# The eight experts of a routed layer: the next expert's tokens gathered one expert ahead, and its first product drawn before the last transposes

## The chip, the cores and the metric

The kernel runs on 1 core of one Trainium2 chip. The metric is device time in microseconds (us). The kernel before takes 2135.12 us, the median of 3 runs (2126.69 to 2139.0).

## The reference

The program is a trunk of two layers on 256 tokens of width 1024, batch 1, in float32. Each layer has a token-mixing half (not touched here) and a channel-mixing half. In layer 0 the latter is a dense SwiGLU; in layer 1 it is routed, and this is where the change lies:

```python
def swiglu(h, w1, w3, w2):
    return (jax.nn.silu(h @ w1) * (h @ w3)) @ w2

def moe_ffn(h, w_router, w1, w3, w2):
    logits = (h @ w_router).astype(jnp.float32)
    top_v, top_i = lax.top_k(logits, TOP_K)          # 2 of 8
    top_w = jax.nn.softmax(top_v, axis=-1)
    gate = jnp.sum(one_hot(top_i, N_EXPERTS) * top_w[..., None], axis=-2)
    y = jnp.zeros_like(h)
    for e in range(N_EXPERTS):
        y = y + gate[..., e:e + 1] * swiglu(h, w1[e], w3[e], w2[e])
    return y
```

Each expert has w1 and w3 of 1024 x 3584 and w2 of 3584 x 1024, in float32: 42 chunks of 1 MiB.

## The kernel before

Each expert works on at most 128 tokens, gathered by a product with a one-hot matrix `sel` (tokens x slots). If an expert is chosen by more than 128 tokens, a second round over all experts follows; in this run there is none, so the expert loop runs 8 times.

**Precision.** Every float32 product is made of three fp32r products: operands are split into a high part (rounded copy, ScalarE, line 1234) and a low part (the difference, VectorE). `mm3` (lines 677 to 679) issues xl·wh, xh·wl, xh·wh. So every weight passes over ScalarE and VectorE once.

**Weights.** SyncE loads chunks of 1 MiB into the ring `raw` of 6 (line 539), each as soon as the chunk six earlier is split. A chunk has two halves of 128x1024. ScalarE copies a half to `w_hi`, VectorE then writes `w_lo` (line 1568); both are rings of 4 halves, so half h can be split only when TensorE has used half h-4 (`half_used`). The splits are written into each engine's instruction order by `use(n)`: it splits up to 3 halves (`AHEAD`) beyond the chunks it takes, then the engine goes on with its other work. ScalarE and VectorE run in their own written order, and whatever stands in it between two splits delays the later one.

**An expert.** Its width 3584 is walked in 7 blocks of 512. The gate product G of a block takes 4 chunk halves (24 matmuls of 128x512) into bank `pA[0]`, the up product U as many into `pA[2]`, the down product 4 halves into the two banks `pO`, in which all 7 blocks accumulate. `silu` (ScalarE, line 1520) reads `pA[0]` into `a_sb`, `hidden` (VectorE, line 2081) multiplies `pA[2]` in, `turn_a` transposes `a_sb` with 4 small matmuls (line 725) into the two banks `pT`, and these are split to `aT_hi`, `aT_lo` (line 2089). Banks `pA[1]` and `pA[3]` are idle in the expert loop.

TensorE's order in one expert is: transpose `sel` to `selT`; open the output banks with a product of zeros; G(0), U(0); then six times G(f), turn_a(f-1), U(f), down(f-1); then `gather` for the next expert (32 matmuls of 128 columns into both `pT`, line 682); turn_a(6); down(6); and the scatter, `selT` times the output `oe` (4 products of 128x512 into `pT`, line 682, each shown as two records).

VectorE's part of it: `one_hot` (line 2051) makes `sel` of the next expert after its first `hidden`; `gathered` (line 2060) scales the gathered tokens out of the banks into `x_f` in 8 instructions, followed by a drain (line 2063); ScalarE and VectorE split `x_f` into `x_hi` and `x_lo` (line 2068); `oe` is copied out half by ScalarE and half by VectorE (line 2109); and four instructions add the scattered rows to `yacc` (line 2114).

Of the kernel before, what the change touches and what calls it, by code (L numbers as in the profile page):

```python
# [31 lines left out]
P = 128  # L32
D = 1024
# [288 lines left out]
def build(nc, a, table, out):  # L322
    ctx = ExitStack()
    with ctx:
# [97 lines left out]
        sel = sb("sel", [P, TT, P], at=work + 20480)  # L422
        selT = sb("selT", [P, TT * P], at=work + 21504)
# [90 lines left out]
        x_ready = sem("x_ready")  # L514
        fin_ready = sem("fin_ready")
# [11 lines left out]
        def _(sp):  # L527
# [56 lines left out]
            for l in range(DEPTH):  # L584
# [37 lines left out]
                else:  # L622
                    def experts():
                        with rounds(sp, 0, NE, {b.raw: EFB * 6}) as e:
                            w1, w3, w2 = (a[n][l // 2].rearrange("e k n -> (e k) n") for n in ("moe_w1", "moe_w3", "moe_w2"))

                            def up(f0):
                                for w in (w1, w3):
                                    for k in range(2):
                                        load(chunk_rows(w, e * D + k * CK * P, f0))  # L630

                            def down(f0):
                                for half in range(2):
                                    load(chunk_rows(w2, e * FFE + f0, half * W))
# [9 lines left out]
                    items = sp.value_load(flag[0:1, 0:1], min_val=NE, max_val=2 * NE)  # L644
                    with sp.If(items > NE):
                        experts()
# [9 lines left out]
        def _(pe):  # L656
# [333 lines left out]
            for l in range(DEPTH):  # L990
# [109 lines left out]
                else:  # L1100
# [16 lines left out]
                    items = pe.value_load(flag[0:1, 0:1], min_val=NE, max_val=2 * NE)  # L1117
                    evacuated(b.A, A_free, 4)
                    G, U, av, xv = Turn(start=FFB + 1), Turn(start=FFB + 1), Turn(start=FFB + 1), Turn()
# [10 lines left out]
                    pe.wait_ge(sel_ready, 2)  # L1130
                    gather()
                    with rounds(pe, 0, items, {b.raw: 42, b.hl: 84, b.T: 22, b.O: 2, G: EFB, U: EFB, av: EFB, xv: 1}):
                        v = xv.take()
                        for t in range(TT):
                            turned([sel[:, t, :]], P)
                        outs = [take_O(), take_O()]
                        for o in outs:
                            mm(o[:, :].rearrange("p (k n) -> p k n", k=CK), zeros[:, :],
                               zeros[:, :].unsqueeze(1).broadcast_to([P, CK, P]), True, False)
                        pe.wait_ge(x_ready, xv.done(v, 2))  # L1140

                        def gate_up(dst, turn, free):
                            v = turn.take()
                            pe.wait_ge(free, turn.done(v - 1))
                            product([dst], lambda j, t: (x_hi[:, j, :], x_lo[:, j, :]), 2)

                        def turn_a():
                            v = av.take()
                            pe.wait_ge(a_ready, av.done(v))
                            for q in range(2):  # L1150
                                turned([a_sb[:, 0, (2 * q + j) * P:(2 * q + j + 1) * P] for j in range(2)], P)

                        def down(last=False):
                            evacuated(b.T, T_free, 2)
                            for half in range(2):
                                for i in range(2):
                                    wh, wl = half_in(i)
                                    for j in range(CK // 2):
                                        k = i * (CK // 2) + j
                                        ins = mm3(outs[half][:, :], aT_hi[:, k, 0:P], aT_lo[:, k, 0:P],  # L1160
                                                  wh[:, j * W:(j + 1) * W], wl[:, j * W:(j + 1) * W], False, last and k == CK - 1)
                                    ins.then_inc(half_used, 1)
                        gate_up(pA[0], G, g_free)
                        gate_up(pA[2], U, u_free)
                        with rounds(pe, 1, EFB, {b.raw: 6, b.hl: 12, b.T: 2, G: 1, U: 1, av: 1}):
                            gate_up(pA[0], G, g_free)
                            turn_a()
                            gate_up(pA[2], U, u_free)
                            down()
                        pe.wait_ge(sel_ready, xv.done(v) + 2)  # L1170
                        gather()
                        turn_a()
                        down(True)
                        evacuated(b.O, O_free, 2)
                        for t in range(TT):
                            for half in range(2):
                                dst = take_T()
                                mm(dst[:, :], selT[:, t * P:(t + 1) * P], oe[:, half * W:(half + 1) * W]).then_inc(T_full, 1)

# [43 lines left out]
        def _(act):  # L1223
# [27 lines left out]
            def start_splits():  # L1251

                b.end = 2 * (DEPTH * MIX_CHUNKS + DENSE_CHUNKS + 6 * EFB)
# [146 lines left out]
            for l in range(DEPTH):  # L1400
# [97 lines left out]
                else:  # L1498
# [4 lines left out]
                    items = act.value_load(flag[0:1, 0:1], min_val=NE, max_val=2 * NE)  # L1503
                    G, xv = Turn(start=FFB + 1), Turn()

                    def hi_x(at):
                        for q in range(2):
                            act.wait_ge(xf_ready, at + q + 1)
                            copy(x_hi[:, 4 * q:4 * q + 4, :], x_f[:, 4 * q:4 * q + 4, :]).then_inc(x_hi_ready, 1)
                    skip(b.T, 2)  # L1510
                    hi_x(0)
                    with rounds(act, 0, items, {b.raw: 42, b.hl: 84, b.hl_in: 84, b.T: 22, b.O: 2, G: EFB, xv: 1}) as e:
                        v = xv.take()
# [3 lines left out]
                        def silu():  # L1517
                            G.take()
                            act.wait_ge(half_used, b.hl.done(b.hl.n - 1))
                            nc.scalar.activation(a_sb[:, 0, :], pA[0][:, :], ACT.Silu).then_inc(g_free, 1)  # L1520

                        def hi_a():
                            for q in range(2):
                                pt, free = T_in()
                                copy(aT_hi[:, 2 * q:2 * q + 2, 0:P], pt[:, 0:SEQ].rearrange("p (k n) -> p k n", k=2)).then_inc(aT_hi_ready, 1)
# [3 lines left out]
                        with rounds(act, 1, EFB, {b.raw: 6, b.hl: 12, b.hl_in: 12, b.T: 2, G: 1}):  # L1529
                            use(2)  # L1530
                            hi_a()
                            silu()
                            use(4)
                        skip(b.T, 2)
                        hi_a()
                        hi_x(xv.done(v, 2))
                        u = use(2)
                        with act.If(e < items - 1):
                            ahead()
                        act.wait_ge(half_used, b.hl.done(u))  # L1540
                        copy(oe[:, 0:W], pO[b.O.slot(b.O.take())][:, :]).then_inc(O_free[0], 1)
                        skip(b.O, 1)
                        skip(b.T, 4)
# [4 lines left out]
        def _(dve):  # L1548
# [42 lines left out]
            def start_splits():  # L1591

                b.end = 2 * (DEPTH * MIX_CHUNKS + DENSE_CHUNKS + 6 * EFB)
# [286 lines left out]
            for l in range(DEPTH):  # L1880
# [127 lines left out]
                else:  # L2008
# [32 lines left out]
                    link(V.tensor_scalar(r(9)[:, 1:2], r(9)[:, 0:1], float(P), float(NE), ALU.is_gt, ALU.mult))  # L2041
                    link(V.tensor_scalar(flag[:, 0:1], r(9)[:, 1:2], float(NE), None, ALU.add))
                    link(V.memset(slot16[:, :, 2 * NE:], -1.0))
                    dve.drain().then_inc(slots_ready, 1)
                    items = dve.value_load(flag[0:1, 0:1], min_val=NE, max_val=2 * NE)
                    av, aq, xv = Turn(start=FFB + 1), Turn(start=2 * FFB + 1), Turn()

                    def one_hot(e):

                        for t in range(TT):  # L2050
                            ins = V.tensor_scalar(sel[:, t, :], iota, slot16[:, t, bass.ds(e, 1)], None, ALU.is_equal)
                        ins.then_inc(sel_ready, 1)

                    def gathered():

                        for q in range(2):
                            pt, free = T_in()
                            for j in range(4):
# [85 lines left out]
```

## Time and profile before

| | |
|---|---|
| profiled execution | 2136.17 us, its span 2134.4 us |
| busy share of the span | PE 93%, PEld 74%, VectorE (DVE) 72%, ScalarE (ACT) 58%, GpSimd (POOL) 4% |
| mean granted TensorE clock | 0.962 of full speed |
| read from HBM | 530.83 MB, 249 GB/s over the span |
| expert phase | from 1024.1 us (first `sel`) to about 2120 us |

PE is TensorE's matmuls, PEld its weight loads. Busy shares are over the whole span. A matmul's record is longer than the distance to the next one, since matmuls overlap in the pipeline, so distances between starts tell the pace. In the timeline, one row can stand for several instructions of a kind (x4), and its duration is from the first start to the last end. What stands in square brackets is idle time of the engine ahead of the row and the engine and line that ended it; DVEq is VectorE's sequencer (here the drain), "issue" means that the profile shows nothing that was waited for.

### The profile page before, as it was taken

The page shows a single profiled execution, that of the slowest core. Times are in us where ns is not written, and L with a number is a line of the kernel's source. Part 1 is how long each engine was busy: PE and PEld are TensorE (multiplying, and loading weights), DVE is VectorE, ACT ScalarE, POOL GpSimd, SP SyncE. Part 2 cuts the span into 40 slices and gives each one's busy share as a digit, 9 for nine tenths or more (in the row PEclk, how much of TensorE's full clock was granted, in tenths as well). Part 3 has the DMA queues.
Part 4 walks back from the last instruction along what each step waited for, and adds up shares of the span by engine and source line. Part 5 has one row for each costly group of instructions (what it writes and reads, how often), then busy time and mean ns, then how long its engine had stood idle before and what let it go on. Part 6 is the DMA issues. An engine that isn't in the chain of part 4 may idle for free.

```text
span 2134.4 us, 28418 instructions
## 1 busy us (share of the span) xinstructions
PE 1991.8 (93%) x9524; PEld 1576.0 (74%) x9524; DVE 1526.7 (72%) x1827; ACT 1237.3 (58%) x1590; POOL 90.3 (4%) x133
## 2 busy tenths in 40 slices
PE   5999999899979999997899999999999999999996
PEld 2777887777767777886686886877868778687785
DVE  2654565654556644656787897988979888798887
ACT  2544454344324544542576876767767677677773
POOL 0510100000003300000000000000000000000000
PEclk7999999899988999998899999999999999999998
DMA  9656545355734655353597997989979989799892
GB/s 324 218 199 216 179 136 160 115 201 186 257 110 157 234 184 216 119 177 99 189 364 275 352 367 260 363 307 316 365 256 365 328 298 366 258 365 345 289 366 101
DMA packets 275180, 532.74 MB, mean 250 GB/s; under 512 B 10720, under 2 KB 23216, under 8 KB 274992
## 3 DMA queue, kind: packets, MB, share of 16 engines
q1 hardware_dynamic: 275120, 531.91, 71.1%
q8 instruction: 41, 0.67, 0.1%
q14 instruction: 19, 0.16, 0.0%
HBM read 530.83 MB, written 1.05 MB: 249 GB/s over the span
## 4 chain that ended last, share of the span: by engine, by line
PE 84%; DVE 8%; ACT 3%; issue 2%; DVEq 2%; SPq 1%; DMA 0%; ACTq 0%
PE pA L677 17%; PE pA L679 17%; PE pA L678 17%; PE pO L682 6%; PE pO L677 6%; PE pO L679 6%; PE pO L678 6%; PE pT L725 4%; PE pT L682 4%; DVE w_lo L1568 2%; ACT w_hi L1234 1%; PE pA L682 1%; SPq L539 1%; DVE yacc L2114 1%; DVEq L2082 1%
## 5 line engine op out<-in xcount | busy, mean ns | idle before, releaser
L1568 DVE TENSOR_TENSOR w_lo<-raw,w_hi 128x1024 fp32r<-128x1024 f32 x914 | 1093.7, 1225 | 311.5 <-ACT w_hi L1234 290.6
L1234 ACT ACTIVATE w_hi<-raw 128x1024 fp32r<-128x1024 f32 x914 | 957.1, 1058 | 566.8 <-PE pA L679 425.0
L677 PE MATMUL pA<-w_hi,x_lo 128*128 128x512 f32 x896 | 360.3, 402 | 1.7 <-DVE x_lo L2068 0.8
L679 PE MATMUL pA<-w_hi,x_hi 128*128 128x512 f32 x896 | 354.3, 395 | 0.0
L678 PE MATMUL pA<-w_lo,x_hi 128*128 128x512 f32 x896 | 354.0, 395 | 0.0
L677 PE MATMUL pA<-w_hi,h_lo 128*128 128x512 f32 (+2 forms) x736 | 300.2, 408 | 8.3 <-DVE w_lo L1568 8.3
L678 PE MATMUL pA<-w_lo,h_hi 128*128 128x512 f32 (+2 forms) x736 | 290.3, 394 | 0.0
L679 PE MATMUL pA<-w_hi,h_hi 128*128 128x512 f32 (+2 forms) x736 | 289.9, 394 | 0.0
L677 PE MATMUL pO<-w_hi,aT_lo 128*128 128x512 f32 x536 | 218.5, 408 | 19.3 <-DVE yacc L1976 8.8
L678 PE MATMUL pO<-w_lo,aT_hi 128*128 128x512 f32 x536 | 216.4, 404 | 0.0
L679 PE MATMUL pO<-w_hi,aT_hi 128*128 128x512 f32 x536 | 216.3, 404 | 0.0
L677 PEld LDWEIGHTS pA<-w_hi,x_lo 128*128 128x128 f32 x896 | 168.4, 188 | 45.3 <-DVE w_lo L1568 4.4
L679 PEld LDWEIGHTS pA<-w_hi,x_hi 128*128 128x128 f32 x896 | 168.5, 188 | 40.8
L678 PEld LDWEIGHTS pA<-w_lo,x_hi 128*128 128x128 f32 x896 | 168.6, 188 | 37.3
L677 PEld LDWEIGHTS pA<-w_hi,h_lo 128*128 128x128 f32 x736 | 142.6, 194 | 52.9 <-issue 18.8
L679 PEld LDWEIGHTS pA<-w_hi,h_hi 128*128 128x128 f32 x736 | 142.3, 193 | 31.8
L678 PEld LDWEIGHTS pA<-w_lo,h_hi 128*128 128x128 f32 x736 | 142.8, 194 | 27.9
L677 PEld LDWEIGHTS pO<-w_hi,aT_lo 128*128 128x128 f32 x536 | 103.8, 194 | 48.0 <-DVE w_lo L1568 10.8
L679 PEld LDWEIGHTS pO<-w_hi,aT_hi 128*128 128x128 f32 x536 | 103.6, 193 | 25.4
L678 PEld LDWEIGHTS pO<-w_lo,aT_hi 128*128 128x128 f32 x536 | 103.9, 194 | 24.5
L1234 ACT ACTIVATE aT_hi<-pT 128x256 fp32r<-128x256 f32 (+1 forms) x123 | 43.8, 401 | 77.3 <-PE pT L725 77.3
L682 PE MATMUL pO<-raw,csilu 128*32 128x512 f32 x384 | 52.9, 665 | 7.4 <-DMA raw<-in_ada_w 7.4
(228 smaller groups left out, 1713.7 us busy)
## 6 DMA issues: line engine op xcount, KB each, us to landing
raw<-in_moe_w SPq DMA_DIRECT2D x336, 1024.0 KB, 6.8
raw<-in_w_in SPq DMA_DIRECT2D x56, 1024.0 KB, 5.9
raw<-in_ada_w SPq DMA_DIRECT2D x48, 1024.0 KB, 9.3
raw<-in_ffn_w SPq DMA_DIRECT2D x33, 1024.0 KB, 6.2
raw<-in_w_out SPq DMA_DIRECT2D x8, 1024.0 KB, 5.1
raw<-in_cmp_k_w SPq DMA_DIRECT2D x4, 1024.0 KB, 5.3
raw<-in_cmp_v_w SPq DMA_DIRECT2D x4, 1024.0 KB, 10.3
raw<-in_w_read_nsa SPq DMA_DIRECT2D x4, 1024.0 KB, 8.4
```

The lines of the kernel that those rows point to most:

```text
L539: sp.dma_start(slot[:, 0:kb * src.shape[2]].rearrange("p (k n) -> p k n", k=kb), src).then_inc(landed[b.raw.slot(g)], 16)
L677: nc.tensor.matmul(dst, xl, wh, start=first, stop=False, skip_group_check=True)
L678: nc.tensor.matmul(dst, xh, wl, start=False, stop=False, skip_group_check=True)
L679: return nc.tensor.matmul(dst, xh, wh, start=False, stop=last, skip_group_check=True)
L682: return nc.tensor.matmul(dst, lhsT, rhs, start=first, stop=last, skip_group_check=True)
L725: ins = nc.tensor.transpose(pt[0:m, i * width:i * width + n], src, ident[0:n, 0:n])
L1234: return nc.scalar.activation(dst, src, ACT.Copy)
L1568: V.tensor_tensor(w_lo[m][:, 0:n], raw[s][:, i * n:(i + 1) * n], w_hi[m][:, 0:n].bitcast(F32), ALU.subtract).then_inc(raw_done, 1)
L2082: dve.drain().then_inc(u_free, 1)
L2114: V.scalar_tensor_tensor(dst, pt[:, :], gate16[:, t, bass.ds(e, 1)], dst, ALU.mult, ALU.add).then_inc(free, 1)
```

## The change

1. TensorE's order. `gather` writes `pA[1]` and `pA[3]` with semaphores of its own, is done one expert further ahead, and stands behind the last down product and ahead of the scatter. The next expert's G(0) stands ahead of turn_a(6), its U(0) behind it: the end of an expert has the same order as any other block. Transposing `sel` and opening the output banks come behind the scatter.
2. `sel` is needed while `gather` is an expert ahead, so there is a second one-hot matrix `sel_s` for the scatter, made by two more VectorE instructions per expert.
3. The splits of the next expert's tokens (`hi_x`, `lo_x`) come behind the U product of block 6, ahead of the splits of the chunks that follow.
4. SyncE loads the next expert's first four chunks ahead of the last two of the present one.
5. The loops: one over passes (one or two), in it one over 7 experts, and the last expert by itself. The branch with which ScalarE and VectorE ended each expert is left only behind the last. In every expert the last of the six blocks stands outside the inner loop.

```diff
@@ SyncE
-                            up(0)
-                            with rounds(sp, 1, EFB, {b.raw: 6}) as f:
-                                up(f * W)
-                                down(f * W - W)
-                            down((EFB - 1) * W)
+                        up(0, 0)
+                        with rounds(sp, 0, NE - 1, {b.raw: EFB * 6}) as e:
+                            blocks(e)
+                            up(e + 1, 0)
+                            down(e, (EFB - 1) * W)
+                        blocks(NE - 1)
+                        down(NE - 1, (EFB - 1) * W)
...
@@ TensorE
                     def gather():
+                        v = gv.take()
+                        pe.wait_ge(sel_ready, gv.done(v) + 1)
+                        pe.wait_ge(gather_free, gv.done(v - 1))
                         for q in range(2):
-                            pt = take_T()
...
-                                    ins = mm(pt[:, j * P:(j + 1) * P], y[:, t, k * P:(k + 1) * P], sel[:, t, :], t == 0, t == 1)
-                            ins.then_inc(T_full, 1)
+                                    ins = mm(pA[1 + 2 * q][:, j * P:(j + 1) * P], y[:, t, k * P:(k + 1) * P], sel[:, t, :], t == 0, t == 1)
+                            ins.then_inc(gather_full, 1)
...
+                        gather()
+                        first_block()
+                        gate_up(pA[2], U, u_free)
+                        gather()
+                        turn_sel()
+                        with rounds(pe, 0, NE - 1, {...}):
+                            blocks()
+                            first_block()
+                            turn_a()
+                            gate_up(pA[2], U, u_free)
+                            down(True)
+                            gather()
+                            scatter()
+                            turn_sel()
+                        blocks()
+                        turn_a()
+                        down(True)
+                        scatter()
...
@@ ScalarE
+                    def hi_x():
+                        v = gv.take()
+                        act.wait_ge(half_used, b.hl.done(b.hl.n - 1))
+                        for q in range(2):
+                            act.wait_ge(xf_ready, gv.done(v, 2) - 1 + q)
+                            copy(x_hi[:, 4 * q:4 * q + 4, :], x_f[:, 4 * q:4 * q + 4, :]).then_inc(x_hi_ready, 1)
...
+                    def block():
+                        use(2)
+                        hi_a()
+                        silu()
+                        use(2)
+
+                    def blocks(more):
+                        with rounds(act, 1, EFB - 1, {...}):
+                            block()
+                            use(2)
+                        block()
+                        if more:
+                            hi_x()
+                        use(2)
...
+                        hi_x()
+                        use(2)
+                        silu()
+                        use(2)
+                        keep_sel()
+                        with rounds(act, 0, NE - 1, {...}):
+                            blocks(True)
+                            block()
+                            use(2)
+                            outs()
+                            keep_sel()
+                        blocks(False)
+                        hi_a()
+                        use(2)
...
@@ VectorE
+                    def blocks(more):
+                        with rounds(dve, 1, EFB - 1, {...}):
+                            block()
+                            use(2)
+                        block()
+                        if more:
+                            lo_x()
+                        return use(2)
...
+                        one_hot(sel, p * NE, sel_ready)
+                        one_hot(sel_s, p * NE, sel_s_ready)
+                        gathered()
+                        one_hot(sel, p * NE + 1, sel_ready)
+                        lo_x()
+                        use(2)
+                        use(2)
+                        hidden()
+                        gathered()
...
+                        with rounds(dve, 0, NE - 1, {...}) as e:
+                            at = p * NE + e
+                            one_hot(sel, at + 2, sel_ready)
+                            dve.wait_ge(T_full, b.T.done(b.T.n - 1))
+                            one_hot(sel_s, at + 1, sel_s_ready)
+                            blocks(True)
+                            block()
+                            outs(use(2))
+                            gathered()
+                            scattered(at)
+                            skip(b.T, 2)
+                        blocks(False)
+                        lo_a()
+                        v = use(2)
...
+                        outs(v)
+                        scattered(p * NE + NE - 1)
```

`block`, `outs` and `scattered` hold the same instructions as before: `block` is the splits, `lo_a` or `hi_a`, and `hidden` or `silu`; `outs` the copy into `oe`; `scattered` the four additions.

## Rows read from the trace of the kernel before

**Rows 1.** What TensorE waited for, 1120 to 2134 us: total us, times, longest.

```profile
PE pT L725 <- DVEq L2063: 10.3, 8, 1.3
```

**Rows 2.** Timeline of TensorE, end of one expert, and next expert's gather: start, duration.

```profile
1284.70 3.73 PE L682 MATMUL pT<-sel,y 128*128 128x128 f32 x32
...
1291.39 0.79 PE L677 MATMUL pO<-w_hi,aT_lo 128*128 128x512 f32 x1 [1.01 <-DVE aT_lo L2089]
...
1294.89 0.39 PE L679 MATMUL pO<-w_hi,aT_hi 128*128 128x512 f32 x1
...
1298.39 0.40 PE L679 MATMUL pO<-w_hi,aT_hi 128*128 128x512 f32 x1
1300.44 4.02 PE L682 MATMUL pT<-oe,selT 128*128 128x512 f32 x8 [1.66 <-issue]
...
1305.87 0.50 PE L677 MATMUL pA<-w_hi,x_lo 128*128 128x512 f32 x1
...
1420.98 3.73 PE L682 MATMUL pT<-sel,y 128*128 128x128 f32 x32
```

**Rows 3.** Timeline of TensorE inside an expert, around the first transposes.

```profile
1184.85 0.40 PE L679 MATMUL pA<-w_hi,x_hi 128*128 128x512 f32 x1
1185.36 0.50 PE L677 MATMUL pA<-w_hi,x_lo 128*128 128x512 f32 x1
...
1186.87 0.60 PE L725 MATMUL pT<-tab,a_sb 128*128 128x128 f32 x4
...
1187.54 0.39 PE L678 MATMUL pA<-w_lo,x_hi 128*128 128x512 f32 x1
```

**Rows 4.** Timeline of all engines, 1148 to 1170 us, the expert before that.

```profile
1148.65 3.73 PE L682 MATMUL pT<-sel,y 128*128 128x128 f32 x32
1150.64 1.37 DVE L2060 TENSOR_SCALAR x_f<-pT,mod 128x128 f32<-128x128 f32 x4 [0.87 <-PE pT L682]
...
1152.43 1.36 DVE L2060 TENSOR_SCALAR x_f<-pT,mod 128x128 f32<-128x128 f32 x4 [0.42 <-PE pT L682]
...
1163.40 0.68 DVE L2109 COPY oe<-pO 128x512 f32<-128x512 f32 x1
...
1166.23 0.30 PEld L682 LDWEIGHTS pT<-oe,selT 128*128 128x128 f32 x2 [0.93 <-DVE yacc L2114]
...
1167.52 1.49 DVE L2114 SCALAR_TENSOR_TENSOR yacc<-pT,gate,yacc 128x512 f32<-128x512 f32 x2 [0.59 <-PE pT L682]
...
1169.57 0.51 PE L677 MATMUL pA<-w_hi,x_lo 128*128 128x512 f32 x1
```

**Rows 5.** Timelines of ScalarE and VectorE in a block in mid-expert.

```profile
1257.26 3.06 ACT L1234 ACTIVATE w_hi<-raw 128x1024 fp32r<-128x1024 f32 x3
...
1262.06 1.06 ACT L1234 ACTIVATE w_hi<-raw 128x1024 fp32r<-128x1024 f32 x1 [0.34 <-PE pA L679]
...
1262.91 0.68 DVE L2081 TENSOR_TENSOR a_sb<-a_sb,pA 128x512 f32<-128x512 f32 x1
1263.86 4.72 DVE L1568 TENSOR_TENSOR w_lo<-raw,w_hi 128x1024 fp32r<-128x1024 f32 x4 [0.26 <-issue]
```

**Rows 6.** Timeline ahead of the first expert's first product: tokens' low part.

```profile
1031.98 1.29 DVE L2068 TENSOR_TENSOR x_lo<-x_f,x_hi 128x512 fp32r<-128x512 f32 x2
```

**Rows 7.** Windows: length, busy us by engine, PEclk, DMA share, GB/s.

```profile
1152.20:1155.30 3.10, 0.85 (x6) 0.37 (x4) 2.21 (x6) 1.31 (x4) 0.00 (x0) 0.93 0.58 218
1155.30:1158.00 2.70, 2.66 (x6) 2.16 (x7) 2.52 (x3) 1.43 (x2) 0.00 (x0) 0.50 0.01 4
...
1162.40:1169.60 7.20, 4.92 (x14) 1.79 (x13) 4.67 (x6) 2.33 (x4) 0.00 (x0) 1.00 0.50 155
...
1180.00:1276.00 96.00, 95.89 (x424) 77.23 (x423) 86.98 (x88) 75.85 (x85) 0.00 (x0) 1.00 1.02 363
```

**Rows 8.** ScalarE's line 1520 from 1010 us on: duration min/median/max, first and last start.

```profile
L1520 ACT ACTIVATE a_sb<-pA x56: 597/606/609, 1040.4 to 2090.1; 128x512 f32<-128x512 f32 x56
L1520 ACT ACT_TABLE_LOAD  x8: 1283/1283/1283, 1039.1 to 1991.2; - x8
```

More of the change, by code:

```diff
@@ new lines, in gather, with turn_sel, gate_up @@
+                            ins.then_inc(gather_full, 1)
+                    def turn_sel():
+                        pe.wait_ge(sel_s_ready, sv.done(sv.take()))
+                        for t in range(TT):
+                            turned([sel_s[:, t, :]], P)
+                    def gate_up(dst, turn, free):
+                        v = turn.take()
+                        pe.wait_ge(free, turn.done(v - 1))
+                        product([dst], lambda j, t: (x_hi[:, j, :], x_lo[:, j, :]), 2)
@@ new lines, in first_block, with turn_a, down @@
+                    def first_block():
+                        pe.wait_ge(x_ready, xv.done(xv.take(), 2))
+                        gate_up(pA[0], G, g_free)
+                    def turn_a():
+                        v = av.take()
+                        pe.wait_ge(a_ready, av.done(v))
+                        for q in range(2):
+                            turned([a_sb[:, 0, (2 * q + j) * P:(2 * q + j + 1) * P] for j in range(2)], P)
+                    def down(last=False):
+                        evacuated(b.T, T_free, 2)
+                        for half in range(2):
+                            for i in range(2):
+                                wh, wl = half_in(i)
+                                for j in range(CK // 2):
+                                    k = i * (CK // 2) + j
+                                    ins = mm3(outs[half][:, :], aT_hi[:, k, 0:P], aT_lo[:, k, 0:P],
+                                              wh[:, j * W:(j + 1) * W], wl[:, j * W:(j + 1) * W], False, last and k == CK - 1)
+                                ins.then_inc(half_used, 1)
@@ L1138, in _, with open_outs @@
+                    def open_outs():
+                        for _ in range(2):
+                            o = take_O()
                             mm(o[:, :].rearrange("p (k n) -> p k n", k=CK), zeros[:, :],
                                zeros[:, :].unsqueeze(1).broadcast_to([P, CK, P]), True, False)
[L1140 to L1162, printed above, removed]
+                    def block():
@@ L1172, in _, with blocks, scatter @@
-                        turn_a()
-                        down(True)
+                        down()
+                    def blocks():
+                        open_outs()
+                        with rounds(pe, 1, EFB - 1, {b.raw: 6, b.hl: 12, b.T: 2, G: 1, U: 1, av: 1}):
+                            block()
+                        block()
+                    def scatter():
                         evacuated(b.O, O_free, 2)
@@ L1514, in _, with silu @@
                         for t in range(TT):
                             T_copy(lambda pt: (selT[:, t * P:(t + 1) * P], pt[:, 0:P]))
[L1517 to L1525, printed above, removed]
+                    def silu():
+                        G.take()
+                        act.wait_ge(half_used, b.hl.done(b.hl.n - 1))
+                        nc.scalar.activation(a_sb[:, 0, :], pA[0][:, :], ACT.Silu).then_inc(g_free, 1)
@@ new lines, in gathered, with lo_x, hidden @@
+                        dve.drain().then_inc(gather_free, 1)
+                    def lo_x():
+                        v = xv.take()
+                        for q in range(2):
+                            dve.wait_ge(x_hi_ready, xv.done(v, 2) - 1 + q)
+                            V.tensor_tensor(x_lo[:, 4 * q:4 * q + 4, :], x_f[:, 4 * q:4 * q + 4, :],
+                                            x_hi[:, 4 * q:4 * q + 4, :].bitcast(F32), ALU.subtract).then_inc(x_ready, 1)
+                    def hidden():
+                        v = av.take()
+                        dve.wait_ge(g_free, av.done(v))
+                        dve.wait_ge(half_used, b.hl.done(b.hl.n - 1))
+                        V.tensor_tensor(a_sb[:, 0, :], a_sb[:, 0, :], pA[2][:, :], ALU.mult).then_inc(a_ready, 1)
+                        dve.drain().then_inc(u_free, 1)
@@ L2094, in _ @@
[L2094 to L2095 removed]
+                    def blocks(more):
+                        with rounds(dve, 1, EFB - 1, {b.raw: 6, b.hl: 12, b.hl_in: 12, b.T: 2, av: 1, aq: 2}):
+                            block()
                             use(2)
[L2097 to L2100 removed]
@@ L2101, in _, with outs @@
-                        gathered()
-                        lo_a()
-                        lo_x(xv.done(xe, 2))
-                        v = use(2)
-                        with dve.If(e < items - 1):
-                            ahead()
+                        block()
+                        if more:
+                            lo_x()
+                        return use(2)
+                    def outs(v):
                         b.O.take()
```

173 lines of the change are left out of this document (79 added, 94 removed).

## The prediction

> **What bounds the kernel now.** I read the page first, then the waits of TensorE, then the timelines around one expert's end, then windows. In the expert phase TensorE is the bound: in 96 us inside an expert it is busy 95.89 us at full clock, with VectorE at 91% of that window, ScalarE at 79%, and DMA moving 363 GB/s at a busy share of 1.02 [rows 7]. The reader should see two things there: only what lies on TensorE's line at an expert's end can be won, and the three others have little room for what the change pushes beside the products. In mid-stream the pace is one 128x512 matmul each 0.2333 us (15 steps from 1294.89 to 1298.39) [rows 2]; I use this pace, not the 0.40 us of a record, because records overlap.
>
> From one gather to the next an expert takes 1420.98 - 1284.70 = 136.28 us [rows 2]. It splits up as:
> - products: 84 halves x 6 matmuls x 0.2333 = 117.6 us;
> - six turn_a inside blocks: from 1186.87 to 1187.54 less one step, 0.44 each [rows 3], 2.6 us;
> - **gap A**, gather and turn_a(6), 1291.39 - 1284.70 = 6.7 us [rows 2]. One wait in it is on VectorE's drain behind `gathered`, since gather and turn_a share both `pT`; 8 of these are 10.3 us [rows 1];
> - **clock**: in 1152.2 to 1155.3, within such a gap, TensorE is busy 0.85 of 3.1 us, and the 2.7 us behind it are granted 0.50, the 1.2 GHz level [rows 7]. The first 8 steps of down(6) take 3.50 us in place of 1.87 [rows 2]: 1.6 us;
> - **gap B**, scatter, turned `sel`, opened banks: from 1298.62 to 1305.87, 7.25 us [rows 2]. No fall of the clock follows it although TensorE is busy for only 4.92 of 7.2 us (granted 1.00) [rows 7];
> - a stall at the first U, 1185.36 against 1185.08 due, 0.3 us [rows 3], and 0.1 for the first step after a pause.
>
> The sum is 136.3, so nothing large is missing.
>
> **Gap A goes.** G(0) of the next expert stands ahead of turn_a(6) and U(0) behind it, as in every block, so turn_a(6) should cost the 0.44 us of the others, its copies hidden by the 5.6 us of U(0). Its products are only moved.
>
> **Gap B grows by the gather.** I count from the end of down(6). TensorE gathers until 3.6 (3.73 less the overlap into the next start [rows 2]). VectorE, beside it: splits behind, then the `oe` copy from 1.05 to 1.75 (1163.40, gap B of that expert having begun 7.25 ahead of 1169.57 [rows 4]). `gathered` starts 2.0 after the gather (1150.64 against 1148.65) and runs 1.37, its second half starts at 3.8 (1152.43) and ends at 5.15 [rows 4]; some 0.3 for the drain, by the 0.26 behind `hidden` [rows 5]: 5.45. Only now can VectorE add the scattered rows, because they are queued behind `gathered`. TensorE has put two scatter products into the two `pT` by then; the third needs the first bank. Addition one ends at 6.2 and the third product starts (as 1166.23 in the old order). The third addition starts 1.3 after that (1167.52) and the last ends at 9.05, and the next product starts 0.56 later, as 1169.57 does behind 1167.52 + 1.49 [rows 4]. So the new gap is 9.6 us. Lower bound 9.0: gather 3.6 and the old 1305.87 - 1300.44 = 5.4 from the first scatter product on [rows 2]. Upper bound 12.7: 5.45 and then the whole of gap B in series. I take 9.6, because each of its links is a row.
>
> **Clock.** In the new gap TensorE works through the first 5.3 us, then it waits in bits of under 1 us. Worst stretch, 5.3 to 8.7: one product of 0.9 and half another and one transpose, over half busy, against 27% ahead of the fall in rows 7 and against gap B (68%) without one. I take no fall; the price if it comes anyway is 1.6 us each.
>
> **`hi_x` and `lo_x`** are moved into block 6, behind U, and the splits of the halves after that are queued behind them. Slack there: U ends about 1261.93 (the `w_hi` copy starts behind it at 1262.06), `hidden` runs at 1262.91, the next `w_lo` starts at 1263.86 and takes a fourth of 4.72, to 1265.05; TensorE needs that half three halves after U's end, 4.2 us, at 1266.13. Slack 1.1 [rows 5]. `lo_x` takes 1.29 [rows 6] and a short issue gap: a stall of 0.2 to 0.5, I take 0.4. ScalarE's two copies are about as long and end ahead of it. If `hidden` starts late there it is up to 1.3; if splits have run ahead, nothing. The stall at the first U, which one_hot behind `hidden` made, should go: both one_hots now stand at the expert's start beside the last additions, and the first split behind them is due only 4.2 us later. 0.3 back.
>
> **SyncE's order, the waits on `gather_free` and `sel_ready`, the dropped branch:** nothing. Loads keep the order of use, and the waits are for work an expert old. DMA: 44.04 MB in the new expert is 337 GB/s on average, under the 363 of the window [rows 7]. The stream between two gaps is as dense as before, so if the ring holds now it holds then; I give it 0, and if DMA could not hold its pace over the one longer stretch, up to 2 us an expert.
>
> **Sum.** New expert: 117.6 + 7 x 0.44 + 9.6 + 0.1 + 0.4 = 130.8 us, 5.5 less. Seven times 38.4, less 1.6 because I count on one of the experts having had no clock fall: about 36.8. The last expert keeps gap B; its gap A and clock, 8.3, become turn_a(6) and the wait for its copies. Bounds 0.44 (all hidden) and 3.1 (gap A without its gather); I take 2.0, since VectorE is busy with splits for about the first 1.05: 6.3 won. Ahead of the first product one_hot stands ahead of `lo_x`: 0.7 lost. Behind U(0) of expert 0 there is a gather of its own with the turned `sel` and the opened banks, which before stood in the shadow of `x_lo`: 3.6 + 0.9 = 4.5 lost. Total 36.8 + 6.3 - 5.2 = 37.9 us. The profiled execution took 2136.17 us (span 2134.4), which makes 2098.3; it is 1 us over the median of the runs, from which it would be 2097.2. I predict 2098 us.
>
> **Rivals.**
> (1) The clock falls in the new gap after all. For it: the gap is longer than either old one, and gathers stood ahead of each fall. Against: the busy shares above. 7 x 1.6 = 11 more: 2109.
> (2) The new gap is in series, 12.7: VectorE, which has `gathered` and the additions back to back, lets TensorE wait, and one_hot and the splits behind it are late too. 7 x 3.1 = 22 more: 2120.
> (3) **Slower:** the new loop structure makes ScalarE load its activation tables inside the blocks. Now 56 silus share 8 loads of 1.28 us, one per pass of the expert loop [rows 8]: the inner loop has none, the top of the expert loop has them. The change splits each inner loop into a loop and a block outside it and nests it in one more loop. If the copies and the silu of each block took a load each, 2.57 us would stand ahead of splits with a slack of 1.1 [rows 5]: a stall of 1.5 in 55 blocks, 83 us, so 2181. It decides from 37.9 / 55 = 0.7 us of stall a block, some 1.8 us of added ScalarE work ahead of its splits; a single load, 0.2 of stall, leaves 2109. Against it: today's inner loop is nested too and stays free, and in the new expert loop both ways in have silu's table.
> On this the Trainium skill speaks against the change: in "ScalarE activation tables: per-element evaluation and per-set limits", section "Table sets in the compiler and the runtime", it says that the back end places the table loads per block. Taken by the letter it would be this rival; the trace, with 8 loads to 56 silus, doesn't show one for each block. The skill's "ScalarE: Activation LUTs", section "What ACT_TABLE_LOAD costs", gives 2.66 us for a switch with its drain; by that estimate two of them would make a stall of some 4 us a block.
> (4) The parts cancel (stalls of splits behind `lo_x`, DMA late by 2 us an expert, gap in series): within 0.5%.
>
> **Chances.** Forecast 0.62, (1) 0.14, (2) 0.10, (3) 0.06, (4) 0.08. A measurement of this kernel can tell about 0.5%, 10.7 us, from no change. Faster by more than that: 0.86; within: 0.08; slower: 0.06. The runs of before spread over 12 us, which I add to the forecast's own bounds (9.0 in the gap and no stall: 2091): low 2087. High 2115: rival 1 in full and part of rival 2.
>
> **What would show it.** From gather to gather 130.8 us; no wait on `gathered`'s drain; 9.6 us from the end of down(6) to the next product, with a wait of about 0.9 ahead of the third scatter product; 0.4 us lost at the first down half of block 6; no 0.50 stretches from 1100 to 2100 us; about 2 table loads in the expert phase in place of 16. It would be wrong if the period were over 134, if ScalarE showed loads in the blocks, or if TensorE waited for `w_lo` in more than one place of an expert.

## The result and the profile after

The changed kernel takes 2102.51 us (median of 4 runs, 2096.96 to 2105.65), the kernel before 2134.57 in the same comparison: ratio 0.9851, 95% interval 0.9815 to 0.9887. Forecast were 2098 us. Run again beside later kernels (`r8_changed_again`, five runs) it gave 2098.16 and a ratio of 0.9822 (0.9799 to 0.9846). The profiled execution has a span of 2101.9 us, 32.5 less than before, where 37.9 were forecast.

The timeline of TensorE at the end of the second expert of the changed kernel, against [rows 2] (start, duration, in brackets the idle time ahead and what ended it):

```profile
1303.49 3.73 PE L692 MATMUL pA<-sel,y 128*128 128x128 f32 x32
1307.06 1.88 PE L692 MATMUL pT<-oe,selT 128*128 128x512 f32 x4
1309.81 1.98 PE L692 MATMUL pT<-oe,selT 128*128 128x512 f32 x4 [0.87 <-DVE yacc L2182]
1311.99 0.30 PE L735 MATMUL pT<-tab,sel_s 128*128 128x128 f32 x1 [0.19 <-DVE yacc L2182]
1312.64 0.33 PE L735 MATMUL pT<-tab,sel_s 128*128 128x128 f32 x1 [0.35 <-DVE yacc L2182]
1313.18 0.60 PE L692 MATMUL pO<-zeros 128*128 128x512 bf16 x2 [0.21 <-issue]
```

Gap A is gone: the gather is followed at once by the scatter. What is left of both gaps is one of 1313.69 - 1303.49 = 10.2 us (the next product starts at 1313.69). The reader should see the 0.87 ahead of the third scatter product, which was forecast as 0.9, and the tail of 1.05 us from the last transpose to the product, of which 0.21 is "issue"; before, it was 0.55 (1305.87 - 1305.32). The gather before stood at 1172.07, so the period is 131.4 us; before it was 136.28 [rows 2].

VectorE in the gap before that one, against [rows 4]. The down product ends at 1172.07, when the gather starts:

```profile
1173.11 0.68 DVE L2175 COPY oe<-pO 128x512 f32<-128x512 f32 x1
1174.06 1.37 DVE L2130 TENSOR_SCALAR x_f<-pA,mod 128x128 f32<-128x128 f32 x4 [0.26 <-PE pA L692]
1175.85 1.37 DVE L2130 TENSOR_SCALAR x_f<-pA,mod 128x128 f32<-128x128 f32 x4 [0.42 <-PE pA L692]
1177.60 1.41 DVE L2182 SCALAR_TENSOR_TENSOR yacc<-pT,gate,yacc 128x512 f32<-128x512 f32 x2 [0.39 <-PE pT L692]
1179.68 1.49 DVE L2182 SCALAR_TENSOR_TENSOR yacc<-pT,gate,yacc 128x512 f32<-128x512 f32 x2 [0.68 <-PE pT L692]
```

This is the chain as forecast: first addition at 5.5 (forecast 5.45), last one ended at 9.1 (9.05).

The windows (length, busy us of PE, PEld, DVE, ACT, POOL, then granted clock, DMA share, GB/s): behind the first product, the gap from the first scatter product on, and nearly the whole expert phase, against [rows 7].

```profile
1035.20:1038.40 3.20, 3.20 (x9) 2.54 (x8) 1.22 (x1) 1.16 (x2) 0.00 (x0) 0.51 0.70 222
...
1175.60:1182.30 6.70, 5.04 (x15) 1.69 (x14) 5.14 (x12) 0.56 (x3) 0.00 (x0) 1.00 0.47 176
...
1060.00:2080.00 1020.00, 1006.29 (x4469) 798.79 (x4468) 903.78 (x951) 758.83 (x855) 0.00 (x0) 1.00 0.93 333
```

No fall of the clock in 1020 us, with one gap of 10.2 us an expert in them. But there is one just behind the very first product, at the 1.2 GHz level, where the kernel before was granted 1.00. Ahead of that product TensorE now waits 3.57 us in one piece, before it waited 1.40 and 0.78 (the kernel before, then the changed one):

```profile
1033.50 0.50 PE L677 MATMUL pA<-w_hi,x_lo 128*128 128x512 f32 x1 [0.78 <-DVE x_lo L2068]
...
1033.91 0.50 PE L687 MATMUL pA<-w_hi,x_lo 128*128 128x512 f32 x1 [3.57 <-DVE x_lo L2139]
```

This fall does not come each time: the same wait of 3.57 us stands in eight of the profiles here, and the clock fell behind it in four; in `r8_changed_again`, which is the same kernel, it did not.

Block 6, where `lo_x` was put, and the last expert, whose transposes have no product to hide behind:

```profile
1152.76 0.40 PE L689 MATMUL pO<-w_hi,aT_hi 128*128 128x512 f32 x1
1153.32 0.50 PE L687 MATMUL pO<-w_hi,aT_lo 128*128 128x512 f32 x1 [0.16 <-DVE w_lo L1636]
...
2074.05 0.60 PE L735 MATMUL pT<-tab,a_sb 128*128 128x128 f32 x4
2075.97 0.50 PE L687 MATMUL pO<-w_hi,aT_lo 128*128 128x512 f32 x1 [1.31 <-DVE aT_lo L2154]
```

A step of 0.56 in place of 0.23, and 0.1 more on the step behind it, is the forecast 0.4; the last expert waits 1.92 in all, forecast 2.0. ScalarE's table loads, against [rows 8]:

```profile
L1563 ACT ACTIVATE a_sb<-pA x56: 598/605/607, 1042.3 to 2063.4; 128x512 f32<-128x512 f32 x56
L1563 ACT ACT_TABLE_LOAD  x1: 1283/1283/1283, 1041.0 to 1041.0; - x1
```

### The profile page after: what moved, and what is told of

It reads as the page before. It is cut to its first block, busy times and chain, and to the rows that moved or that the text cites. A ratio compares the mean times of both kernels' runs of the same rounds, so it can differ in the third digit from the quotient of the medians.

```text
span 2101.9 us, 28303 instructions
## 1 busy us (share of the span) xinstructions
PE 1977.0 (94%) x9524; PEld 1567.4 (75%) x9524; DVE 1524.3 (73%) x1841; ACT 1218.4 (58%) x1574; POOL 89.4 (4%) x133
## 3 DMA queue, kind: packets, MB, share of 16 engines
HBM read 530.83 MB, written 1.05 MB: 253 GB/s over the span
## 4 chain that ended last, share of the span: by engine, by line
PE 85%; DVE 8%; ACT 3%; issue 2%; DVEq 1%; DMA 1%; SPq 0%; ACTq 0%
PE pA L687 18%; PE pA L689 18%; PE pA L688 18%; PE pO L692 7%; PE pO L687 6%; PE pO L689 5%; PE pO L688 5%; PE pT L735 4%; DVE w_lo L1636 2%; PE pT L692 2%; PE pA L692 2%; ACT w_hi L1277 1%; DMA raw<-in_ada_w 1%; DVE yacc L2182 1%; DVEq L2147 0%
## 5 line engine op out<-in xcount | busy, mean ns | idle before, releaser
L687 PE MATMUL pO<-w_hi,aT_lo 128*128 128x512 f32 x536 | 213.9, 399 | 13.7 <-DVE yacc L2044 8.8
```

What stands on the lines that cost most here:

```text
L687: nc.tensor.matmul(dst, xl, wh, start=first, stop=False, skip_group_check=True)
```

## The experiments

Each label is a kernel of its own. Where a run is named against the changed kernel, the period from gather to gather and the gap are read from its profile, since the times of one kernel spread over some 6 to 13 us. Not all parts were undone one by one: the order of SyncE's loads was only changed together with TensorE's, and the dropped branch not at all.

No edit touches what stands ahead of the first gather, and yet that gather starts anywhere from 1015.3 to 1028.4 us in the profiles. So the medians of two kernels can differ by some us that the edit did not make. The time from the first gather to the end of the span is free of this (us, profiled executions):

| before | changed | r8 (changed again) | r4 | r1 | r2 | r3 | r5 | r6 | r7 | r9 |
|---|---|---|---|---|---|---|---|---|---|---|
| 1109.5 | 1077.1 | 1075.9 | 1105.8 | 1095.9 | 1076.6 | 1071.4 | 1073.0 | 1057.1 | 1053.4 | 1251.7 |

The whole 32 us of the change lie in this part.

### r4_own_banks_only: one part of the change alone

```diff
@@ the kernel before, gather
-                            pt = take_T()
...
-                                    ins = mm(pt[:, j * P:(j + 1) * P], ...)
-                            ins.then_inc(T_full, 1)
+                                    ins = mm(pA[1 + 2 * q][:, j * P:(j + 1) * P], ...)
+                            ins.then_inc(gather_full, 1)
```

> The kernel before with one part alone: gather writes the idle banks pA[1] and pA[3], with its own semaphores; its place and VectorE's order are as before. The waits view puts 10.3 us (8 times 1.3) of TensorE's idle time on the drain behind gathered. Theory (VectorE does gathered ahead of lo_a in any case, so the product waits for it wherever the bank is): gap A from 6.7 to some 6.3, total 3 less, 2131, and the clock still falls behind it. Rival (the shared banks are the price): gap A 5.4, total 10 less or, if the clock doesn't fall either, 22 less.

Measured: 2128.65 us against 2130.84, ratio 0.9991 (0.9973 to 1.001), no difference that can be told. The wait on the drain is gone from the waits of TensorE, and another stands in its place (1060 to 2090 us):

```profile
PE pO L679 <- DVE aT_lo L2091: 15.3, 7, 2.2
PE pT L684 <- issue: 11.6, 7, 1.7
```

Gap A is 3.57 + 2.78 = 6.35 us in place of 6.7, as the theory had it: VectorE does `gathered` ahead of `lo_a`, and that order, not the bank, was most of the price. The banks alone are worth 0.35 us an expert, by the trace only. In windows over this gap and behind it:

```profile
1144.50:1150.90 6.40, 4.22 (x38) 3.96 (x36) 4.79 (x12) 2.38 (x5) 0.00 (x0) 1.00 0.84 311
1150.90:1154.00 3.10, 3.10 (x7) 2.45 (x8) 2.18 (x3) 0.54 (x2) 0.00 (x0) 0.50 0.00 1
```

The clock falls behind it as before (behind 6 of 8 experts; before 7 of 8).

### r1_transposes_first: the order around the last transposes undone

```diff
@@ the changed kernel, TensorE
                             blocks()
-                            first_block()
                             turn_a()
-                            gate_up(pA[2], U, u_free)
                             down(True)
                             gather()
                             scatter()
                             turn_sel()
+                            first_block()
+                            gate_up(pA[2], U, u_free)
```

The orders of the other three engines and of the loads are turned back with TensorE's.

> The changed kernel with one part undone: turn_a(6) and down(6) stand ahead of the next expert's G(0) and U(0) again, which come behind the scatter; gather banks, lookahead and loops are kept. My theory (turn_a(6) costs only its 0.44 us when a product hides its copies, and some 1.9 us when it doesn't, as in the last expert of the changed kernel): 1.5 us more at each of 7 experts, and up to 0.3 more of stall since both one_hots stand behind hidden again. Period 133.0, total some 2114. Rival (this order alone is what removed gap A of 6.7 us and the clock's fall): 5 us or more an expert, total 2138 or more. Rival 2 (nothing, the copies were never on the path): total 2102.

Measured: 2112.03 us, ratio 0.9898 (0.987 to 0.9926). From gather to gather 133.65 us, 2.2 more than the changed kernel, where I had 1.5 to 1.8.

```profile
1286.46 0.60 PE L735 MATMUL pT<-tab,a_sb 128*128 128x128 f32 x4
1289.14 0.50 PE L687 MATMUL pO<-w_hi,aT_lo 128*128 128x512 f32 x1 [2.07 <-DVE aT_lo L2157]
```

The bare transposes cost 2.68 us, against 1.92 in the last expert, where no `lo_x` had put VectorE behind just before. VectorE's `lo_a` begins 1.77 us behind the transposes here, after a row of splits that `x_lo` had pushed back, and 1.04 us behind them in the last expert. So the new order is worth 2.2 us of the 4.9 won per expert, and a little more by the clock, which fell behind two of these seven gaps: 7 x 2.2 and 2 x 1.6 are 18.6 us, and from the first gather on this kernel takes 18.7 more than the changed one. Of the other 2.7 us, 1.6 are the fall of the clock that followed 7 of 8 such gaps before, and 1.1 is that the two gaps are 2.7 + 10.2 us here and were 6.7 + 7.25. How that 1.1 is shared between the moved gather and VectorE's order no run shows.

### r2_open_early: the tail of the gap

```diff
@@ the changed kernel, TensorE
                     def blocks():
-                        open_outs()
...
                             scatter()
+                            open_outs()
                             turn_sel()
```

> The changed kernel with one line moved: the output banks are opened ahead of the turned sel, not behind it at the top of the expert loop. Theory (the new gap is 10.2 us in place of 9.6 because the loop's branch now falls between the last transpose and the opening products, where nothing hides it; opened early, the two products fill a wait for VectorE's additions): gap 9.7 us, 0.5 less, total 3.5 less, 2099. Rival (the entry into the inner loop costs it): gap within 0.1 of 10.2, total 2102.

Measured: 2103.58 us, ratio 0.9849 (0.9809 to 0.9889); the gap 10.1 us. The theory falls: the opening products now hide beside an addition, and the idle time only moves behind the last transpose.

```profile
1311.74 0.33 PE L735 MATMUL pT<-tab,sel_s 128*128 128x128 f32 x1 [0.31 <-DVE yacc L2183]
1312.72 0.50 PE L687 MATMUL pA<-w_hi,x_lo 128*128 128x512 f32 x1 [0.66 <-issue]
```

TensorE waits for nothing that the profile shows for 0.66 us between the last transpose and the product. In that place stand the outer loop's end and start and the inner loop's start; which of them costs how much, and whether they are the cause at all, stays open.

### r3_adds_first: VectorE's order in the gap

```diff
@@ the changed kernel, VectorE
-                            gathered()
                             scattered(at)
+                            gathered()
```

> The changed kernel with VectorE's order turned round in the gap: the four scattered additions first, gathered behind them. Theory (VectorE's series of gathered and additions sets the gap): the third scatter product waits less, gap 10.2 - 0.65 = 9.55 us, total some 4.5 less, 2098; VectorE is 2 us later at its first split of the block, which still fits (due 4.2 us behind the restart). Rival (that lateness comes back as a wait for w_lo in the first block): the same gap less 0.65 but a stall of 0.5 to 1 there, total 2102 or above.

Measured: 2098.39 us, ratio 0.9843 (0.9812 to 0.9873). The gap is 9.4 us, 0.8 less, and the period is 130.9, 0.5 less:

```profile
1296.82 3.73 PE L692 MATMUL pA<-sel,y 128*128 128x128 f32 x32
...
1306.20 0.50 PE L687 MATMUL pA<-w_hi,x_lo 128*128 128x512 f32 x1
```

The time alone does not tell this kernel from the changed one (ratio 0.9843 against 0.9851 and 0.9822); the trace does. The series of VectorE's work did set the gap. Its lateness just fits: the waits show nothing new for `w_lo`, but the fourth half of the first block comes 0.1 us late with 0.1 more on the next step, so 0.2 of the 0.8 are lost again.

### r5_sel_early: TensorE's gap shortened without VectorE's

```diff
@@ r3, TensorE
                             down(True)
+                            turn_sel()
                             gather()
                             scatter()
-                            turn_sel()
```

With it, VectorE's `one_hot` for `sel_s` comes to stand between the additions and `gathered`, and ScalarE copies `selT` out right behind its half of `oe`.

> As r3 (additions ahead of gathered), and the turned sel moved from behind the scatter to ahead of the gather, where the banks pT are free and its copy lies beside the gather. Theory: TensorE no longer waits for the third and fourth addition, gap 9.4 - 1.1 = 8.3 us; but VectorE now has additions, gathered and one_hots in series until 12.5 us, its first split ends at 13.7, and TensorE needs it at 8.3 + 4.2 = 12.5: a new wait for w_lo of some 1.2 us in the first block, so no gain over r3: 2098. Rival (VectorE has the slack): period 1.1 less than r3, total 2091.

Measured: 2101.11 us, ratio 0.9835 (0.9813 to 0.9857), beside 2098.16 for the changed kernel run with it: nothing gained. The gap is 7.8 us (1303.49 to 1311.33), 1.5 less than in r3, and the period 130.9, as in r3. VectorE and, below, the product that waits for it:

```profile
1312.34 2.63 DVE L2129 TENSOR_SCALAR x_f<-pA,mod 128x128 f32<-128x128 f32 x8
1315.64 0.48 DVE L2119 TENSOR_SCALAR sel<-tab,slot 128x128 f32<-128x128 f32 x2 [0.67 <-issue]
1316.14 4.63 DVE L1635 TENSOR_TENSOR w_lo<-raw,w_hi 128x1024 fp32r<-128x1024 f32 x4
...
1317.42 0.50 PE L687 MATMUL pA<-w_hi,x_lo 128*128 128x512 f32 x1 [1.54 <-DVE w_lo L1635]
```

The shorter gap comes back as a step of 1.93 us in the first block: three halves are split ahead, and the fourth waits for VectorE. The wait is 1.5 us where some 1.2 were expected.

### r6_interleaved: the same work in another order

```diff
@@ r5, TensorE
-                            gather()
-                            scatter()
+                            gather([0])
+                            scatter([0])
+                            gather([1])
+                            scatter([1])
@@ r5, VectorE
-                            scattered(at)
-                            one_hot(sel_s, at + 1, sel_s_ready)
-                            gathered()
+                            scattered(at, [0])
+                            gathered()
+                            scattered(at, [1])
+                            one_hot(sel_s, at + 1, sel_s_ready)
```

> As r5, but TensorE interleaves: half of the gather, two scatter products, the other half, two scatter products; VectorE adds two, then gathered, then adds two. Theory: no bank is waited for, gap 8.0 us, VectorE ready for its first split at 10.4, which ends at 11.6, due at 12.2, so no wait for w_lo: period 129.3, total 15 less than the changed kernel, 2087. Rival (VectorE's series is the bound of the boundary whatever the order): gap or a w_lo stall make up for it, 2098.

Measured: 2084.34 us, ratio 0.9751 (0.9728 to 0.9774), 13.8 less than the changed kernel run with it.

```profile
1303.21 1.95 PE L692 MATMUL pA<-sel,y 128*128 128x128 f32 x16
1305.00 1.88 PE L692 MATMUL pT<-oe,selT 128*128 128x512 f32 x4
1306.72 1.95 PE L692 MATMUL pA<-sel,y 128*128 128x128 f32 x16
1308.50 1.88 PE L692 MATMUL pT<-oe,selT 128*128 128x512 f32 x4
1310.22 0.59 PE L692 MATMUL pO<-zeros 128*128 128x512 bf16 x2
1310.47 0.59 PE L687 MATMUL pA<-w_hi,x_lo 128*128 128x512 f32 x1
```

Not one bracket: TensorE never waits. The gap is 7.5 us (1302.99 to 1310.47), the period 128.8, and no `w_lo` wait comes with it. Most of what this wins over r5 is not in the gap, which is only 0.4 shorter, but in VectorE: its first split starts 9.7 us behind the end of the down product (1312.71), in r5 12.7 us (1316.14), because it has less to wait for between its pieces of work. Seven times 2.6 us of period are 18 us, and from the first gather on this kernel takes 18.8 less than the changed one; the medians show 13.8 of them. The 0.66 of "issue" is gone too: where nothing is waited for ahead of it, no such idle time shows.

### r7_split_tokens: the last stall

```diff
@@ r6, VectorE (ScalarE's hi_x in the same way)
                         block()
-                        if more:
-                            lo_x()
-                        return use(2)
+                        use(1)
+                        if more:
+                            lo_x([0])
+                        v = use(1)
+                        if more:
+                            lo_x([1])
+                        return v
```

> As r6, and the splits of the next expert's tokens are cut in two: first half behind the splits of the first chunk of the down product, second half behind those of the second chunk; TensorE waits for each half by itself. Theory (the 0.43 us ahead of the first down half of block 6 is lo_x standing in front of a split with 1.1 us of slack; two pieces of 0.7 each fit): that stall goes, period 0.4 less, total 2 to 3 less than r6. Rival (the slack is used up by the pieces too): a stall of 0.2 to 0.5 at other halves, total as r6.

Measured: 2075.15 us, ratio 0.9715 (0.9688 to 0.9743), the fastest of all. The period is 128.3, 0.4 less than r6, and the `w_lo` wait is gone. TensorE's waits for `pO` from 1060 to 2070 us, in r6 and then here:

```profile
PE pO L687 <- DVE aT_lo L2156: 1.3, 1, 1.3
PE pO L687 <- DVE w_lo L1638: 1.2, 7, 0.2
...
PE pO L687 <- DVE aT_lo L2169: 1.3, 1, 1.3
```

By the period this is 3 us in 7 experts, and from the first gather on the two profiles are 3.7 us apart. The 9 us between the medians are more than the edit explains; the runs of this kernel alone spread over 13 us.

### r9_table_loads: table loads put into each block

The changed kernel with one line more in ScalarE's `block`; its result is used nowhere. Two runs.

```diff
                         hi_a()
+                        nc.scalar.activation(spare[:, :], ones[:, 0:1], ACT.Sqrt)
                         silu()
```

> The changed kernel with one Sqrt of 128x1 ahead of each silu in the blocks, its result unused, so that ScalarE loads two tables in each block: the slower rival, made on purpose. Theory by the prediction (2.57 us of loads and 0.2 for the Sqrt ahead of splits with a slack of 1.1): a stall of 1.5 to 1.7 us in each of 55 blocks, 83 to 95 us more: 2185 to 2197. By the skill's 2.66 us for a switch with its drain (ScalarE: Activation LUTs, What ACT_TABLE_LOAD costs): some 4.3 us a block, 2340. Rival (ScalarE has 3 us of idle time a block that take the loads up): under 20 us more, below 2122.

Measured: 2272.47 us, ratio 1.0651 (1.061 to 1.0692), 170 us over the changed kernel. ScalarE, then TensorE in the block:

```profile
1200.97 1.28 ACT L1574 ACT_TABLE_LOAD   x1
1202.26 0.20 ACT L1574 ACTIVATE spare<-tab 128x1 f32<-128x1 f32 x1
1202.47 1.28 ACT L1564 ACT_TABLE_LOAD   x1
1203.77 0.60 ACT L1564 ACTIVATE a_sb<-pA 128x512 f32<-128x512 f32 x1
...
1206.62 0.50 PE L688 MATMUL pA<-w_hi,x_lo 128*128 128x512 f32 x1 [1.94 <-DVE w_lo L1638]
```

The stall is a step of 2.34, so 2.1 us, and 0.1 on the next step: 55 x 2.2 = 121 us. The window behind it shows the second cost, the clock at its lower level:

```profile
1206.60:1210.20 3.60, 3.58 (x9) 2.79 (x10) 3.60 (x4) 2.56 (x3) 0.00 (x0) 0.57 0.63 198
```

The timeline has 35 such stretches behind 55 stalls, and the granted clock averages 0.95 from 1060 to 2245 us, which is some 118 us at half speed or 3.4 for each. At some 1.6 us each (the price in the prediction) they cost 56 us. Together 177, near the 170 measured and the 174.6 by which this kernel is longer from the first gather on. Theory and rival both missed the size; a load pair costs 1.28 + 1.28 and nothing beside it on ScalarE. The Trainium skill (ScalarE: Activation LUTs, What ACT_TABLE_LOAD costs) gives 1283 ns for the load, which the rows agree with, and 2.66 us for a switch with its drain, which does not show here.

## Why the prediction was right, step by step

- **Gap A goes:** right. The order is worth 2.2 us an expert (r1), own banks alone 0.35, too little for the time to show (r4). What [rows 1] names as the wait was not the price by itself: without it the next wait, for `aT_lo`, grows from 1.0 to 2.2 us.
- **Gap B grows to 9.6:** the chain of VectorE was right to 0.1 us; the size was 10.2. The failed term is "the next product starts 0.56 later": it was 1.1. TensorE's loop ends now fall between the last transposes and the product, for which the prediction has no term; that they are the cause is read from the order and not shown, since r2 only moved the idle time. Seven times 0.6 is 4.2 us of the 5.4 missing, the start below is 0.7, and 0.5 stay open.
- **Clock:** no fall in the new gap, right; the price of the seven old falls came back.
- **The start:** from the first `sel` to the first product of G(1) in the first expert it was 20.7 us and is 26.6, so 5.9 were lost in place of 5.2. That this is near is luck: the wait ahead of the first product cost 0.3 and not 0.7, the gather of its own 4.0 and not 4.5, and one fall of the clock behind the first product, 1.5 us, was not foreseen and does not come in each execution.
- **`lo_x` in block 6:** 0.43 measured, 0.4 forecast; r7 takes it away.
- **The stall at the first U and SyncE's order:** the stall is gone; no wait for a load appears. Two things in the prediction are not right here. The stalled product (1185.36) is the last half of G(1), not U. And `one_hot` need not be the cause: in the kernel before, a table load of 1.28 us also stood ahead of the expert's first `silu` [rows 8] and pushed the splits back. r1 has both `one_hot`s behind `hidden` and no such load, and lost 0.1 us there. Which of the two made the 0.3 was not tested.
- **Last expert:** 1.92 against 2.0.
- **Slips in the working:** the listed parts of the old expert add up to 136.2 and not 136.3, and the lower bound of 2087 does not follow from the 2091 and the 12 us that it is said to be made of. Neither changes the forecast.
- **Rivals:** (1) did not come. (2) came neither in the gap nor in the first block, but r5 shows that it was near: 1.5 us less gap than r3 and the whole gain is back in a wait. (3) did not come: 2 table loads in the expert phase in place of 16. That fits the argument that a loop needs none where all ways into it have the same table, though no run tests the argument. The Trainium skill says that the back end places the table loads per block (ScalarE activation tables: per-element evaluation and per-set limits, Table sets in the compiler and the runtime); taken by the letter, as in the prediction, the trace does not agree, with one load to 56 silus. r9 shows that the mechanism, where it comes, makes the kernel slower, and twice as much as I had worked out: 2.77 us of added work made a stall of 2.1, so the slack behind silu is 0.7 us and not 1.1, and the clock, which the price left out, fell behind 35 of 55 stalls.

## What to carry to other kernels

Where one engine is the bound, read the gap as a series on two engines: work out when TensorE is free again and when the helper engine's first due item is ready, and shorten both, since shortening one alone (r5) gave nothing and ordering the same work for both (r6) gave 14 us over the changed kernel. A wait in the profile is worth what it lasts only if nothing else on the same engine is late next: 10.3 us of drain waits were worth under 3 (r4). Small helper work goes in pieces no longer than the slack at its place (r7).

## What the runs showed of the hardware

The granted clock falls not only with a long gap. These are the stretches in which TensorE waited, and how often the clock fell to its lower level right behind them:

| what TensorE did before | run | times the clock fell |
|---|---|---|
| one wait of 3.57 us ahead of the first product | eight profiles | 4 of 8 |
| gather, then one wait of 2.2 us | r4 | 6 of 8 |
| gather, then waits of 1.3 and 1.0 us | before | 7 of 8 |
| dense products, one wait of 2.1 us behind bare transposes | r1 | 2 of 7 |
| dense products, one wait of 1.95 us | r9 | 35 of 55 |
| dense products, one wait of 1.7 us, then the scatter with one of 0.4 | before, r4 | 0 of 14 |
| dense products, one wait of 1.6 us | r5 | 0 of 7 |
| gaps of 7.5 to 10.2 us, no wait over 0.9 us | changed, r8, r1, r2, r3, r6, r7 | none |

The length of the gap does not order these rows, and the waits in it come nearer to it. The longest single wait does not do it alone either: two of 1.3 and 1.0 us brought the clock down where one of 1.7 did not. What an idle stretch costs is therefore its length and up to 1.6 us more.
